# A paged K cache: two of four pages per sample transposed in 32x32 blocks by VectorE instead of by TensorE

## What is computed

```python
def page_step(state, phys):
    o_acc, carry = state
    kp = cache_k[phys]
    vp = cache_v[phys]
    zp = sb_logits(q, kp, sb_bias)
    o_p, carry = sb_block(zp, True, vp, carry)
    return (o_acc + o_p, carry), None

(o, _), _ = lax.scan(page_step, (o, carry), page_table.T, reverse=True)
```

## Time and profile before

| | |
|---|---|
| median of 3 runs | 1241.37 us (1241.24 to 1241.98) |
| the profiled execution's own time | 1240.57 us |
| its span, first to last instruction | 1238.9 us |
| mean granted TensorE clock, share of full speed | 0.965 |
| TensorE matmuls busy | 1129.2 us (91%) |
| TensorE weight loads busy | 989.1 us (80%) |
| VectorE busy | 628.8 us (51%) |
| ScalarE busy | 399.6 us (32%) |
| GpSimd busy | 408.1 us (33%) |
| DMA | 220.69 MB, mean 178 GB/s |
| K pages: loads, each | 256 of 256 KB |

### The profile page before, as it was taken

How to read it: one execution, slowest core, us unless ns; L and a number is a source line. 1 busy time by engine, 2 the same in 40 slices (tenths; PEclk the granted TensorE clock), 3 DMA queues, 4 the chain that set the end, 5 groups by cost and what they waited for, 6 DMA issues and landing times.

```text
span 1238.9 us, 25950 instructions
## 1 busy us (share of the span) xinstructions
PE 1129.2 (91%) x9815; PEld 989.1 (80%) x9815; DVE 628.8 (51%) x853; ACT 399.6 (32%) x626; POOL 408.1 (33%) x341
## 2 busy tenths in 40 slices
PE   6679999989887899899979887899999999999997
PEld 2358879867656677667769866899999999999996
DVE  0463633555534776566469554854554002554543
ACT  2532332324434554554441344412121111211121
POOL 0133343424322253334433102333333333332330
PEclk9879999989978999999989999999999999999998
DMA  9526685855899699989853131332222222222222
GB/s 363 176 85 236 222 314 199 315 179 192 284 358 340 203 339 309 357 302 348 270 207 121 35 118 53 103 103 68 85 76 76 79 93 86 83 78 66 64 64 76
DMA packets 126409, 220.69 MB, mean 178 GB/s; under 512 B 9935, under 2 KB 68564, under 8 KB 126308
## 3 DMA queue, kind: packets, MB, share of 16 engines
q1 hardware_dynamic: 103010, 146.10, 34.4%
q0 software_dynamic: 20480, 67.13, 15.4%
q10 hardware_dynamic: 2818, 6.13, 1.4%
HBM read 213.52 MB, written 5.80 MB: 177 GB/s over the span
## 4 chain that ended last, share of the span: by engine, by line
PE 77%; DVE 10%; DMA 5%; ACT 3%; issue 2%; SPq 2%; ACTq 0%; POOLq 0%; POOL 0%; DVEq 0%
PE ps L512 36%; PE ps L1547 14%; PE ps L1628 8%; PE ps L573 4%; PE ps L1653 4%; DMA k_page<-in_cache_sb_k 3%; PE ps L1685 3%; PE ps L1503 2%; DVE h_lo L417 2%; DVE run L1328 1%; DVE aw L1334 1%; PE ps L356 1%; DMA v_late<-in_cache_sb_v 1%; PE ps L1664 1%; DVE r_sum L675 1%
## 5 line engine op out<-in xcount | busy, mean ns | idle before, releaser
L468 POOL TENSOR_TENSOR w_lo<-w_raw,w_hi 128x2048 fp32r<-128x2048 f32 (+3 forms) x49 | 192.5, 3930 | 397.6 <-ACT w_hi L445 358.5
L512 PE MATMUL ps<-h_hi,w_hi 128*128 128x288 f32 x832 | 179.7, 298 | 11.6 <-DVE h_lo L417 8.4
L512 PE MATMUL ps<-h_lo,w_hi 128*128 128x288 f32 x832 | 178.6, 297 | 0.0
L512 PE MATMUL ps<-h_hi,w_lo 128*128 128x288 f32 x832 | 178.5, 296 | 0.0
L1628 PE MATMUL ps<-cc,k_page 128*128 128x128 f32 x1024 | 145.1, 295 | 32.4 <-DVE kT L1301 12.9
L1628 PEld LDWEIGHTS ps<-cc,k_page 128*128 128x128 f32 x1024 | 121.1, 150 | 54.7 <-issue 37.9
L445 ACT ACTIVATE w_hi<-w_raw 128x2048 fp32r<-128x2048 f32 (+3 forms) x47 | 77.9, 1662 | 257.8 <-PE ps L512 227.2
L609 POOL DMA_DIRECT2D v_late<-in_cache_sb_v x168 | 90.3, 537 | 177.1 <-issue 109.2
L512 PEld LDWEIGHTS ps<-h_hi,w_hi 128*128 128x128 f32 x832 | 134.5, 189 | 12.8 <-issue 9.3
L1301 DVE COPY kT<-ps 128x512 f32<-128x512 f32 x128 | 87.8, 691 | 95.2 <-PE ps L1628 94.8
L512 PEld LDWEIGHTS ps<-h_lo,w_hi 128*128 128x128 f32 x832 | 134.5, 189 | 0.0
(11 more groups left out here) (253 smaller groups left out, 1853.5 us busy)
## 6 DMA issues: line engine op xcount, KB each, us to landing
k_page<-in_cache_sb_k SPq DMA_DIRECT2D x256, 256.0 KB, 5.2
v_late<-in_cache_sb_v POOLq DMA_DIRECT2D x168, 256.0 KB, 5.2
v_early<-in_cache_sb_v POOLq DMA_DIRECT2D x88, 256.0 KB, 4.9
mw_raw<-in_w_in SPq DMA_DIRECT2D x12, 1024.0 KB, 5.8
w_raw<-in_w_gate SPq DMA_DIRECT2D x11, 1024.0 KB, 5.3
w_raw<-in_w_up SPq DMA_DIRECT2D x11, 1024.0 KB, 5.3
w_s<-in_w_in SPq DMA_DIRECT2D x4, 1536.0 KB, 12.8
w_raw<-in_w_down SPq DMA_DIRECT2D x8, 768.0 KB, 4.4
```

What stands on the lines that cost most here:

```text
L468: return nc.gpsimd.tensor_tensor(w_lo[s][:, ks, :], w_raw[s][:, ks, :], w_hi[s][:, ks, :].bitcast(F32), ALU.subtract)
L512: op = nc.tensor.matmul(ps[:, 2 * t + hf, 0:b - a], weights[s][:, k, t * P:(t + 1) * P], x[:, k0 + k, a:b], start=begin and k == ks[0] and ...
```

## The change

Of each sample's four pages per chunk, the first two (x = 0, 1) take a new way; the other two stay as they are, with two PSUM banks instead of three.

- SyncE loads a page of the new way into the 32 partitions of one quadrant of `k_quad` (quadrant 2x + s for sample s), four keys to a partition at distance 32, as four pieces of 2 KB. The four such loads of a chunk stand ahead of its four other pages, and the first waits until VectorE has transposed the chunk before (`s_kqt`).
- VectorE transposes `k_quad` (128 x 2 x 512 per instruction, two instructions per chunk) in blocks of 32x32 into `kTq`, behind its copies of the chunk.
- TensorE multiplies `kTq` with `q_blk`, a copy of the queries laid out by blocks of 32 features: 32 matmuls of 64 rows, 32 output partitions and 128 keys, into the end of bank 2 and the start of bank 3. The old score matmuls shrink to 256 keys.
- ScalarE's sigmoids read across the two banks. The scan works in place in `om_s`; `run_s` is gone.

```diff
@@
-        k_page = at("k_page", [8, CH], R_M)
+        k_quad = at("k_quad", [4, CH], R_M)
+        k_page = at("k_page", [4, CH], R_M + 8192)
...
-        kT = at("kT", [2, HP, SEQ], R_W + 16384)
+        kT = at("kT", [2, HP, 2 * P], R_W + 16384)
+        kTq = at("kTq", [2 * HEADS, P], R_W + 24576)
@@
         def k_pages(sp, C):
 
-            for q in range(8):
+            if C:
+                sp.wait_ge(s_kqt, 2 * C)
+            for s in range(2):
+                for x in range(2):
+                    page = page_of(sp, C, 4 * s + x)
+                    r = 32 * (2 * x + s)
+                    sp.dma_start(k_quad[r:r + 32, :, :],
+                                 ck[0, bass.ds(page, 1)].rearrange("o (a i) h d -> i (o a) (h d)", a=4)).then_inc(s_kq, 16)
+            for n in range(4):
                 if C:
-                    sp.wait_ge(s_ktr, 8 * C + q - 7)
-                load_page(sp, C, q, ck, k_page[:, q:q + 1, :], s_kp[q // 2])
+                    sp.wait_ge(s_ktr, 4 * C + n - 3)
+                load_page(sp, C, 4 * (n // 2) + 2 + n % 2, ck, k_page[:, n:n + 1, :], s_kp[n // 2])
@@
             def sample_sigmoids(S, w):
                 act.wait_ge(m_["score"], S + 1)
-                act.wait_ge(m_["weight"], S)
-                nc.scalar.activation(beta_s[:, 0:w], ps[:, 3, 0:w], ACT.Sigmoid, scale=SB_SCALE,
+                if S:
+                    G, k = divmod(S - 1, 9)
+                    act.wait_ge(m_["run"], 19 * G + 3 + 2 * k)
+                scores_ = ps[:, 2:4, :].rearrange("p b n -> p (b n)")
+                scores_ = scores_[:, SEQ:SEQ + w] if w == NS else scores_[:, 3 * P:7 * P]
+                nc.scalar.activation(beta_s[:, 0:w], scores_, ACT.Sigmoid, scale=SB_SCALE,
@@
             step(dve, nc.vector.memset(q_bd[:, :, :, :], 0.0))
+            step(dve, nc.vector.memset(q_blk[:, :, :], 0.0))
@@
             def copy_k(C):
-                for q in range(1, 8, 2):
-                    if q == 1 and C:
+                for n in (1, 3):
+                    if n == 1 and C:
                         dve.wait_ge(m_["score"], 9 * ((C - 1) // 8) + (C - 1) % 8 + 2)
-                    dve.wait_ge(s_ktr, 8 * C + q + 1)
-                    nc.vector.tensor_copy(kT[:, q // 4, :, (q % 4) * P:(q % 4 + 1) * P], tiled(ps[:, q % 3, :]))\
-                        .then_inc(m_["k_copied_d"], 1)
+                    dve.wait_ge(s_ktr, 4 * C + n + 1)
+                    nc.vector.tensor_copy(kT[:, n // 2, :, P:2 * P], tiled(ps[:, 1, :])).then_inc(m_["k_copied_d"], 1)
+
+            def transpose_quadrants(C):
+
+                slots = kTq[:, :, :].rearrange("p b (a i) -> p a b i", a=4)
+                dve.wait_ge(s_kq, 64 * (C + 1))
+                for a in (0, 2):
+                    nc.vector.transpose(slots[:, a:a + 2, :, :], k_quad[:, a:a + 2, :].rearrange("p a (b j) -> p a b j", j=32))\
+                        .then_inc(s_kqt, 1)
@@
                 op.then_inc(m_["queries"], 1)
+                blocks = q_blk[:, :, :].rearrange("p (j h e) n -> p j h e n", h=2, e=2)
+                for s in range(2):
+                    for x in range(2):
+                        to = 32 * (2 * x + s)
+                        for h2 in range(2):
+                            for e in range(2):
+                                r = 64 * h2 + 32 * e
+                                op = nc.vector.tensor_copy(
+                                    blocks[to:to + 32, :, h2, e, 16 * s + 8 * h2:16 * s + 8 * h2 + 8],
+                                    pT[r:r + 32, T_Q:T_Q + HP, SEQ + 16 * G + 8 * s:SEQ + 16 * G + 8 * s + 8])
+                op.then_inc(m_["queries"], 1)
@@
                     if C + 1 < CHUNKS:
                         copy_k(C + 1)
+                        transpose_quadrants(C + 1)
@@
             def k_transposes(C):
                 items_copied(max(C - 1, 0))
-                for q in range(8):
-                    pe.wait_ge(s_kp[q // 2], 32 * (C + 1))
-
-                    last = (q - 3) if q >= 3 else (6, 7, 5)[q] - 8
-                    if C or last >= 0:
-                        pe.wait_ge(m_["k_copied_a" if last % 2 == 0 else "k_copied_d"], 4 * C + last // 2 + 1)
+                for n in range(4):
+                    pe.wait_ge(s_kp[n // 2], 32 * (C + 1))
+                    if C or n >= 2:
+                        pe.wait_ge(m_["k_copied_d" if n % 2 else "k_copied_a"], 2 * C + n // 2)
                     for j in range(HP):
-                        op = nc.tensor.transpose(ps[:, q % 3, j * P:(j + 1) * P], k_page[:, q, j * P:(j + 1) * P], ident)
+                        op = nc.tensor.transpose(ps[:, n % 2, j * P:(j + 1) * P], k_page[:, n, j * P:(j + 1) * P], ident)
                     op.then_inc(s_ktr, 1)
@@
-                pe.wait_ge(m_["k_copied_a"], 4 * C + 4)
-                pe.wait_ge(m_["k_copied_d"], 4 * C + 4)
+                pe.wait_ge(s_kqt, 2 * C + 2)
...
+                for x in range(2):
+                    r = slice(64 * x, 64 * x + 64)
+                    for i in range(4):
+                        for j in range(HP):
+                            nc.tensor.matmul(ps[32 * j:32 * j + 32, 2 + x, (3 - 3 * x) * P:(4 - 3 * x) * P], q_blk[r, 4 * j + i, :],
+                                             kTq[r, 4 * j + i, :], start=i == 0, stop=i == 3)
+                pe.wait_ge(m_["k_copied_a"], 2 * C + 2)
+                pe.wait_ge(m_["k_copied_d"], 2 * C + 2)
                 for s in range(2):
                     for j in range(HP):
-                        op = nc.tensor.matmul(ps[32 * j:32 * j + 32, 3, :], q_bd[:, s, j, :], kT[:, s, j, :],
+                        op = nc.tensor.matmul(ps[32 * j:32 * j + 32, 3, P:3 * P], q_bd[:, s, j, :], kT[:, s, j, :],
                                               start=s == 0, stop=s == 1)
```

More of the change, by code:

```diff
@@ L258, in hybrid_layer @@
                                               "rows", "rows_tr", "rows_copied")}
-        s_kp = [sem(f"k_pages{i}") for i in range(4)]
+        s_kp = [sem(f"k_pages{i}") for i in range(2)]
+        s_kq, s_kqt = sem("k_quadrants_loaded"), sem("k_quadrants_transposed")
         s_v1 = [sem(f"v_early_pages{i}") for i in range(V1 // 2)]
@@ L1018, in copy_k @@
             def copy_k(C):
-                for q in range(0, 8, 2):
-                    if q == 0 and C:
+                for n in (0, 2):
+                    if n == 0 and C:
                         act.wait_ge(m_["score"], 9 * ((C - 1) // 8) + (C - 1) % 8 + 2)
-                    act.wait_ge(s_ktr, 8 * C + q + 1)
-                    nc.scalar.activation(kT[:, q // 4, :, (q % 4) * P:(q % 4 + 1) * P], tiled(ps[:, q % 3, :]),
-                                         ACT.Copy).then_inc(m_["k_copied_a"], 1)
+                    act.wait_ge(s_ktr, 4 * C + n + 1)
+                    nc.scalar.activation(kT[:, n // 2, :, 0:P], tiled(ps[:, 0, :]), ACT.Copy).then_inc(m_["k_copied_a"], 1)
             def sample_sigmoids(S, w):
                 act.wait_ge(m_["score"], S + 1)
-                act.wait_ge(m_["weight"], S)
-                nc.scalar.activation(beta_s[:, 0:w], ps[:, 3, 0:w], ACT.Sigmoid, scale=SB_SCALE,
+                if S:
[4 more added lines that the diff above has]
+                nc.scalar.activation(beta_s[:, 0:w], scores_, ACT.Sigmoid, scale=SB_SCALE,
                                      bias=bias_s[:, 0:1])
-                nc.scalar.activation(om_s[:, 0:w], ps[:, 3, 0:w], ACT.Sigmoid, scale=-SB_SCALE,
+                nc.scalar.activation(om_s[:, 0:w], scores_, ACT.Sigmoid, scale=-SB_SCALE,
                                      bias=bias_s[:, 1:2]).then_inc(m_["om"], 1)
@@ L1307, in weights @@
                 if w == NS:
-                    nc.vector.memset(run_s[:, w:w + 1], 1.0).then_inc(m_["run"], 1)
+                    nc.vector.memset(om_s[:, w:w + 1], 1.0).then_inc(m_["run"], 1)
                     dve.wait_ge(m_["run"], R + 1)
                     R = R + 1
-                nc.vector.tensor_tensor_scan(run_s[:, 0:w][:, ::-1], om_s[:, 0:w][:, ::-1], om_s[:, 0:w][:, ::-1],
-                                             run_s[:, w:w + 1], ALU.mult, ALU.bypass).then_inc(m_["run"], 1)
+                om_ = om_s[:, 0:w][:, ::-1]
+                nc.vector.tensor_tensor_scan(om_, om_, om_, om_s[:, w:w + 1], ALU.mult, ALU.bypass).then_inc(m_["run"], 1)
                 dve.wait_ge(m_["run"], R + 1)
@@ L1317, in weights @@
                     step(dve, nc.vector.memset(beta_s[:, NS:P], 0.0))
-                nc.vector.tensor_tensor(beta_s[:, 0:w], beta_s[:, 0:w], run_s[:, 1:w + 1], ALU.mult)\
+                nc.vector.tensor_tensor(beta_s[:, 0:w], beta_s[:, 0:w], om_s[:, 1:w + 1], ALU.mult)\
                     .then_inc(m_["weight"], 1)
                 dve.wait_ge(m_["weight"], S + 1)
-                nc.vector.tensor_copy(run_s[:, SEQ:SEQ + 1], run_s[:, 0:1]).then_inc(m_["run"], 1)
+                nc.vector.tensor_copy(om_s[:, SEQ:SEQ + 1], om_s[:, 0:1]).then_inc(m_["run"], 1)
```

(5 more changed lines are left out.)

13 lines of the change are left out of this document (9 added, 4 removed).

## The result

The changed kernel takes **1335.91 us** (median of four runs, 1329.84 to 1338.34) against 1241.67 for the kernel before beside it (1241.24 to 1244.5): a ratio of 1.0743, 95% interval 1.0711 to 1.0776. It is slower, as forecast, but by 94 us and not by 25, and it lies above the range.

The account below looks back on a forecast made before the run. Early steps were taken as TensorE-bound, late ones as bound by no single engine but, after the change, by a 15.7 us K-load ring. -4 early, +3 boundaries, +21 late steps, +5 extra loads: +25 on 1240.6, 1266 us; range 1240 to 1300.

Parts of the forecast that it names:

- the ring: K loads: next chunk's first quadrant load waits for this chunk's block transposes; 15.7 us floor per chunk step, +21 us late.
- The signs named beforehand: Late steps nearly equal near 15.7 us; SyncE waiting for block transposes; TensorE idle some 40 us before k_page transposes.
- landing of the last page: Ring term: the last K page's load lands in 3.2 us with no V load beside it; 2.5 least, 5.2 median.
- two pages through TensorE: Ring term: TensorE transposes two pages sharing a semaphore, 1.1 us, a quarter of the earlier block's time.
- restart: Ring term: from block transposes done to SyncE's first issue, with the page number's read, 0.7 us.
- the 5 us for extra loads: Two late steps of 17.40 and 23.90 us, queues crowded by extra loads and stores: half their 9.9 us excess kept.
- The load shape: Rival: K loads into 32 partitions land 0.4 us slower each, ring 17.3 us, 30 us more, 1296 us; chance 0.15.
- Its sign: Slow-landing rival's sign in the profile: k_quad's landing well over k_page's.
- new 32 matmuls: TensorE's added score matmuls of 32 by 128 per chunk: 1.9 us, 59 ns each.
- The 0.17 us charged for a change of array shape: TensorE: one more array shape change per chunk, 0.17 us ahead of the weight load, 5 us over 31 chunks.
- sixteen new query copies: VectorE, per group: 175 ns each, 2.9 us; hidden in the first two groups, +3 us in all at two late boundaries.
- The ring does not close: Rival: late steps set by VectorE's 15.3 us cycle, shortened some 1.3 us each to near 13.3; 1215 us, chance 0.13.

Follow-up runs that it names:

- e5: Kernel before, with one wait added: SyncE's first K load of a chunk waits for VectorE's last kT copy of the chunk before; 1287.92 us.
- e4: Changed kernel, with VectorE making the two block transposes of every chunk twice; 1401.02 us.
- e6: Changed kernel, with V loads from the thirteenth late page on cut to 64 of 512 columns; 1306.09 us.
- e8: Kernel before, with four of eight K pages per chunk loaded in four pieces into one 32-partition quadrant each; 1296.42 us.
- e9: Kernel before, with the waits of e8 but plain loads into 128 partitions; 1243.29 us.
- e7: Changed kernel, with page loads issued ahead of quadrant loads and the latter as plain 128-partition loads; 1255.71 us, repeated at 1255.49.
- e1: Changed kernel, with SyncE issuing a chunk's four page loads ahead of its four quadrant loads; 1287.11 us.
- e3: Changed kernel, with quadrant loads turned into plain 128-partition loads, same queue place and waits; 1332.79 us.
- e10: e7 with block transposes cut to a quarter of their columns from the second chunk on; 1237.66 us.

## Why the prediction was wrong in size

**Right: the place and the kind.** All but 2 us lie in the late steps, and they are set by the ring the prediction drew, piece by piece. e5 builds the same ring without any of the new work and pays 46 us. e4 lengthens it and each late step follows. The signs named beforehand came: SyncE's wait for the block transposes, TensorE's wait for k_page about 40 us (36.8), late steps closer together than before though not nearly equal (16.2 to 23.4 us from K transpose to K transpose, 10.6 to 23.9 before).

**The step that failed is the sum of the ring: 15.7 us forecast, 18.9 measured.** Two of its terms were too small, the landing of the last page (3.2 against 5.2 us) and the two pages through TensorE (1.1 against 2.0). Term by term, for the turn above:

| term | forecast | measured |
|---|---|---|
| eight issues | 7.7 | 7.9 |
| landing of the last page | 3.2 | 5.2 |
| two pages through TensorE | 1.1 | 2.0 |
| kT copy | 0.7 | 0.7 |
| block transposes | 2.3 | 2.3 |
| restart | 0.7 | 0.7 |

That turn is a typical one. The chain has seventeen turns of the ring between 334 and 715 us: their landings run from 3.9 to 12.7 us with a median of 5.2, and TensorE's two pages took 1.9 to 2.0 us in fourteen of them and 1.1 in three.

*Landing.* "POOL issues its eight V loads ahead of this window, so I take 3.2" was read from the order of the kernel before. A slower ring moves the V sums too, and these free the V slots. In the changed kernel POOL's timeline has all eight V loads in the very window in which the last K pages land (656.25 to 664.8 us):

```profile
656.48 0.55 POOL L616 DMA_DIRECT2D v_late<-in_cache_sb_v  x1
...
664.56 0.54 POOL L616 DMA_DIRECT2D v_late<-in_cache_sb_v  x1 [0.62 <-issue]
```

e6 takes most of V's bytes away and the landing is 3.2 again. The median of the earlier trace rows, 5.2, which I kept for the range, was the right value, as the seventeen turns show: a landing's time belongs to what runs beside it after the change.

*TensorE.* I took a quarter of the early block of the earlier trace rows, 128 ns a transpose. In the ring TensorE has stood idle for the page and runs at the lower of its two clock levels. Stretches of the changed kernel:

```profile
659.60:664.80 5.20, 1.20 (x8) 0.88 (x8) 2.01 (x4) 0.60 (x1) 2.39 (x5) 0.82 1.00 351
664.80:666.80 2.00, 1.98 (x9) 1.98 (x10) 0.00 (x0) 0.60 (x1) 0.29 (x1) 0.50 0.83 279
```

It was busy 1.20 of 5.20 us, and its eight transposes then ran at a granted clock of 0.50, that is 1.2 GHz: 1.98 us. The earlier trace rows had shown late steps at 0.71 and 0.79, and I didn't price it. The first of the two rows also shows DMA full (1.00 at 351 GB/s) while the pages land.

With 18.9 in place of 15.7 the prediction's own formula gives 19 x 3.2 = 61 us more, 1327. The last 9 us to 1336 are steps longer than such a turn: the twenty late ones average 19.55. The two with landings of 12.66 and 6.95 us are in them; the 5 us for extra loads in the prediction's sum was meant for steps like these, though for others. I have no run that attributes the rest.

**The load shape: a rival priced at half.** The prediction gave slow 32-partition loads 0.4 us each from x_tok's 3.6 us landing, and added 30 us to the ring. x_tok fills 64 partitions and landed alone; a landing alone says little of what loads take from one another. e8 against e9 shows 0.75 us of all DMA engines a load. The rival's mechanism is real, 53 us in the kernel before and 31 in e7 against e1, but in the changed kernel it is mostly hidden: e3 gains 3 us. Its sign didn't come either: k_quad landed in 3.9 us and k_page in 4.3. Ring and shape are two limits on the same loads, and removing one uncovers the other, which is why e1 alone gave back only half. The page SBUF — State Buffer of the Trainium skill (Door 1: The DMA port swizzle) says that 32 partitions reach 8 of 16 ports, which would at most double what such a load takes. The runs agree with that as an estimate: four loads are 1.05 of the 4.9 MB of a 20.3 us step at 242 GB/s, 21%, and at twice the share for these e9's 0.70 becomes 0.85, which is e8's.

**TensorE's and VectorE's terms.** The new 32 matmuls took 1.56 us (64 records, in the chain at 709.50) and not 1.9, so ordinary early steps fell from 20.3 to 19.5 us, twice the 0.4 forecast. The 0.17 us charged for a change of array shape is not shown by its row: the same gap stands ahead of K transposes in the earlier trace rows, where the shape does not change. Block transposes took 1.22 us each where I had 1.15, and the bounds for two, 1.9 to 2.8, held.

The early gain is lost again at the group boundary. The step over it grew from 31.0 to 37.0 us (the next one shrank from 20.3 to 17.6). The prediction gave this step nothing, and called the sixteen new query copies of 175 ns hidden there. They were not. The kT copy, two block transposes, twenty query copies and two evacuations stand in one row on VectorE. The chain of waits runs along that row for 12.2 us, from 236.88 to 249.12, and a projection tile of TensorE waits for its end. Two of the copies took far longer than 0.17 us, and the tile behind them was slow:

```profile
239.92 2.78 DVE q_bd L1374
...
245.39 2.30 DVE q_blk L1385
...
249.26 8.44 PE ps L1586 x48
```

GpSimd's timeline has an instruction beside each of the two, and each copy ended within 0.05 us of it:

```profile
240.25 2.40 POOL L944 TENSOR_TENSOR mw_lo<-mw_raw,mw_hi 128x1024 fp32r<-128x1024 f32 x1
...
245.33 2.33 POOL L944 TENSOR_TENSOR mw_lo<-mw_raw,mw_hi 128x1024 fp32r<-128x1024 f32 x1 [1.66 <-ACT mw_hi L1020]
```

No copy into `q_bd` took over 0.18 us in the kernel before. That these two were held up by GpSimd is what the times suggest; no run isolates it. The tile of 8.44 us took 6.6 before; the granted clock over it was 0.76, and 1.00 before. The same step is 37.3 us in e7 and 31.6 in e10: 1.6 of the 5.7 us between them are the shorter block transposes, 2.0 are query copies (8.4 us against 6.4, with two long ones against one) and 2.1 are the tile (8.70 against 6.62). The two late boundaries took 78.6 us for their four steps against 71.4, +7 where I had +3 (that difference holds what the ring adds to them).

**"The ring does not close"**, 1215 us, is out: it closes, and where e7 opens it and removes the load shape too, the time is 1255, not 1215. That rival left out VectorE: in e7 the scores wait for its block transposes, and e10, with a quarter of them, is 18 us faster. Even then the late steps are 14.7 us and not the rival's 13.3, so its saving behind the kT copy did not come either.

In short, taken away one after another from the changed kernel: load shape -3 (e3), ring -77 (e7), three quarters of the block transposes -18 (e10), which ends at 1237.7. In the other order the ring alone is -49 (e1) and the shape then -31 (e7). So 28 of the 94 us (80 together, less 49 and 3) have no place of their own; they belong to ring and shape together.

## What to carry to other kernels

When a load's slot is freed by a step that stands behind the last load of the same queue, add up the whole circle, issues and landing included, before counting what each engine saves: here it outweighed a TensorE saving of 0.8 us a step. Price its pieces as they will be inside the circle: transfers with whatever else gets shifted beside them, and TensorE at the granted clock that follows idle time, not at that of a busy stretch. Call small copies hidden only after looking at what stands behind them in their queue, and at what else runs beside them. And a load into few partitions should be judged by the DMA share it takes at the same GB/s where DMA is at 0.9 already, not by how fast a lone one lands.

## What the hardware showed

- Four of eight K loads a chunk into 32 partitions each, rather than 128, raised the DMA share from 0.70 to 0.85 at the same 242 GB/s, and cost 53 us (4%) once the share had no room (e8, e9).
- A block transpose of 128x1024 f32 on VectorE in 32x32 blocks took 1.22 us, 1.19 ns an element of each partition, where a copy of 512 elements from PSUM took 1.35 (691 ns): per element it is the cheaper one.
- Eight TensorE transposes of 128x128 f32 took 1.98 us at a granted clock of 0.50, against 4.10 for 32 in a busy stretch.
- VectorE copies of the queries (64x32 and 32x32 f32) took 0.17 us as a rule, but 2.78 and 2.30 us where GpSimd's 128x1024 TENSOR_TENSOR ran, and ended within 0.05 us of it. Two cases in the changed kernel's trace; not isolated.
- A wait alone can lower the clock. In e5, with the matmuls of the kernel before, the late stretch (316.8 to 657.7 us) has the granted clock at 0.90 against 0.94, and TensorE's busy time rose with it:

```profile
316.80:657.70 340.90, 277.89 (x3038) 212.75 (x3038) 177.37 (x272) 143.22 (x273) 108.22 (x172) 0.90 0.82 271
```

277.89 us against 263.04 for the same work: a stall is paid a second time in slower matmuls behind it.
